# Five early expert rows of the first tile added by VectorE onto the residual, and one row given back to TensorE

## The reference

```
qry    = (x_blk @ w_query).reshape(T, 8, 2, 128)
scores = einsum('thpd,hpnd->thpn', qry, sub_keys)
top_s, top_i = top_k(scores, 16)              # for either half of the key
best_s, pos  = top_k(cand_s, 16)              # over the 16 x 16 sums
gate = softmax(best_s)
act  = gelu(einsum('thkd,td->thk', expert_u[idx], x_blk))
ff   = einsum('thk,thkd->td', gate * act, expert_v[idx])
h    = h + ff
```

## Time and profile before

| | |
|---|---|
| median of 3 runs | 1584.37 us (1582.99 to 1586.37) |
| the profiled execution, its own time | 1583.33 us |
| its span in the trace | 1581.4 us |
| busy: PE, DVE, ACT, POOL | 1346.1, 972.3, 537.5, 564.5 us |
| mean granted TensorE clock | 0.966 of full speed |
| read from HBM | 618.38 MB, mean 392 GB/s over the span |

### The profile page before, as it was taken

One profiled execution on the slowest core, in us unless ns is written; L12 is line 12 of the kernel. 1 busy time (PEld: TensorE's weight loads), 2 busy tenths in 40 slices (PEclk: granted clock), 3 DMA queues, 4 the chain that ended last, 5 costly groups with the idle time before them and its releaser, 6 DMA issues.

```text
span 1581.4 us, 14465 instructions
## 1 busy us (share of the span) xinstructions
PE 1346.1 (85%) x4096; PEld 664.7 (42%) x4096; DVE 972.3 (61%) x2428; ACT 537.5 (34%) x1638; POOL 564.5 (36%) x532
## 2 busy tenths in 40 slices
PE   7999899889776997889998699788899877777776
PEld 5555565445332443333555244333365432222222
DVE  3327598988774434763477856574557887554544
ACT  2324332323233223562323323564322323332322
POOL 1001345454442332444443333344444343333330
PEclk9999999999997999989999899999999999999998
DMA  9317999999999999999999999999999999999995
GB/s 380 145 53 293 377 408 421 421 421 420 421 421 422 421 420 422 419 402 410 421 421 420 422 420 421 421 405 396 422 421 420 421 421 421 423 421 422 421 422 212
DMA packets 85086, 620.39 MB, mean 392 GB/s; under 512 B 10352, under 2 KB 10352, under 8 KB 11280
## 3 DMA queue, kind: packets, MB, share of 16 engines
q0 software_dynamic: 74768, 551.65, 84.4%
q1 hardware_dynamic: 9792, 67.77, 10.4%
q10 hardware_dynamic: 448, 0.05, 0.0%
HBM read 618.38 MB, written 1.05 MB: 392 GB/s over the span
## 4 chain that ended last, share of the span: by engine, by line
PE 41%; DMA 39%; DVE 10%; ACT 7%; issue 3%; SPq 0%; POOL 0%; ACTq 0%; DVEq 0%; POOLq 0%
DMA arena<-in_peer_uv_dram,hnT 28%; PE banks L542 25%; PE banks L567 5%; PE banks L422 5%; DMA raw<-in_peer_uv_dram,hnT 5%; DMA work<-in_peer_uv_dram,hnT 4%; DVE arena L1422 3%; PE banks L688 2%; DMA rt<-in_diff_lambda_k_dram 2%; ACT g_e L930 2%; ACT hnT L919 1%; PE banks L514 1%; DVE raw L1422 1%; DVE work L1422 1%; ACT hnT L914 1%
## 5 line engine op out<-in xcount | busy, mean ns | idle before, releaser
L542 PE MATMUL banks<-arena,g_e 128*128 128x512 f32 x1184 | 575.5, 619 | 129.7 <-ACT g_e L930 128.7
L348 POOL DMA_INDIRECT arena<-in_peer_uv_dram,hnT x299 | 324.8, 1086 | 508.2 <-PE banks L542 498.4
L542 PEld LDWEIGHTS banks<-arena,g_e 128*128 128x128 f32 x1184 | 217.8, 196 | 404.8 <-issue 213.0
L1422 DVE CUSTOM_DVE_ANT_0 arena<-arena,hrows 128x1024 f32<-128x1024 f32 x209 | 253.9, 1222 | 153.9 <-DMA arena<-in_peer_uv_dram,hnT 149.8
L914 ACT ACTIVATE hnT<-hnT 128x2 f32<-128x2 f32 (+1 forms) x240 | 48.7, 203 | 697.0 <-DVE hnT L1422 692.2
L542 PE MATMUL banks<-raw,g_e 128*128 128x512 f32 x424 | 208.2, 622 | 41.3 <-ACT g_e L930 37.3
L348 POOL DMA_INDIRECT raw<-in_peer_uv_dram,hnT x106 | 115.8, 1092 | 178.2 <-PE banks L542 175.8
L930 ACT ACTIVATE g_e<-ident,hnT 128x128 f32<-128x128 f32 x501 | 172.7, 393 | 1.7 <-ACT hnT L919 0.6
L1422 DVE CUSTOM_DVE_ANT_0 arena<-arena,banks 128x1024 f32<-128x1024 f32 x90 | 109.6, 1220 | 85.4 <-DMA arena<-in_peer_uv_dram,hnT 85.3
L542 PEld LDWEIGHTS banks<-raw,g_e 128*128 128x128 f32 x424 | 78.3, 197 | 135.1 <-issue 78.4
L1422 DVE CUSTOM_DVE_ANT_0 raw<-raw,hrows 128x1024 f32<-128x1024 f32 x80 | 97.6, 1225 | 56.3 <-DMA raw<-in_peer_uv_dram,hnT 55.9
(11 more groups left out here) (236 smaller groups left out, 1299.5 us busy)
## 6 DMA issues: line engine op xcount, KB each, us to landing
arena<-in_diff_in_dram SPq DMA_DIRECT2D x24, 1024.0 KB
arena<-in_peer_query_dram SPq DMA_DIRECT2D x16, 1024.0 KB
arena<-in_gla_in_dram POOLq DMA_DIRECT2D x5, 2048.0 KB, 21.1
arena<-in_peer_query_dram SPq DMA_DIRECT2D x4, 2048.0 KB, 10.3
arena<-in_diff_out_dram SPq DMA_DIRECT2D x8, 1024.0 KB
arena<-in_peer_uv_dram,hnT POOLq DMA_INDIRECT x299
work<-in_gla_out_dram POOLq DMA_DIRECT2D x2, 2048.0 KB, 40.1
arena<-in_gla_in_dram SPq DMA_DIRECT2D x2, 1024.0 KB, 12.2
```

Source lines behind the costliest of these rows:

```text
L348: pool.indirect_dma_start(pair(n), None, table, bass.IndirectOffsetOnAxis(ap=places[:, o:o + 1].bitcast(u32), axis=0)).then_inc(S(f"pair_l ...
L542: last = nc.tensor.matmul(bank(2 * (tile % NT) + half), diags[:, slot * P:(slot + 1) * P], v_row(n)[:, half * 512:(half + 1) * 512], start ...
L1422: V.tensor_tensor_reduce(out=u_row(n), in0=u_row(n), in1=normed, scale=1.0, scalar=0.0, op0=ALU.mult, op1=ALU.add, accum_out=dots[:, o:o + ...
```

## The change

Rows 1, 3, 5, 7 and 9 join `ADDED`, and row 16 leaves it. Nothing else is edited, but everything that is computed from the list follows: the diagonals that ScalarE makes, the rows that TensorE sums, the semaphore and count on which the gathers 8, 10, 14, 16, 18 and 25 wait (these take over the buffers of rows 1, 3, 5, 7, 9 and 16), the wait of `add_experts`, and the slots of the diagonals.

```
--- before.py
+++ after.py
@@ -132,7 +132,7 @@
 
 
 HOME, TURNS, BEFORE = homes()
-ADDED = [n for n in range(16, 80, 6)]
+ADDED = [1, 3, 5, 7, 9] + [n for n in range(22, 80, 6)]
 SUMMED = [n for n in range(ROWS) if n not in ADDED]
```

## The result

The changed kernel took 1586.44 us, median of 22 runs (1583.98 to 1589.83), against 1583.74 us (1581.61 to 1589.21) for 22 runs of the kernel before: ratio 1.0018, 95% interval 1.0012 to 1.0023, so 2.9 us slower and just under the 0.2% taken as no change. The forecast was 1585.4 on a median of 1584.37, +1.1 us. The profiled execution took 1586.36 us with a span of 1584.3, 2.9 above the span of before.

The account below looks back on a forecast made before the run. The gathers' DMA stream up to about 226 us was taken as the bound. Gather 26's data flowing 0.8 us later and gather 27's 0.3 summed to +1.1 us: 1585.4 us on the median (+0.07%), range 1581.7 to 1587.8.

Parts of the forecast that it names:

- The adds cost nothing: VectorE's five added adds, 1.33 us each, 6.7 us in all, are covered by waits: 0 on the path.
- Their buffers, 0: Gather 10 waits for add 3 (165.0 instead of 163.16), gather 18 for add 9; nothing runs dry: 0.
- Rows 1, 3 and 9 save nothing: On TensorE these rows precede waits for diagonals, so removing them only leaves idle gaps of 5.3 and 3.1 us.
- Row 16, +1.72: Row 16 returns to TensorE in front of row 17 and puts rows 17, 18 and 19 1.72 us late.
- The price of a fall, 1.75 us: TensorE's half clock behind each new gap lasts four matmuls and costs 1.75 us; bounds nothing and 3.1 us.
- half clock for longer: Rival, chance 0.13: on TensorE the second gap, or both, costs 3.1 us instead of 1.75; 1586.8 to 1588.2 us.
- A rule weighed, nothing for the adds' effect on POOL: A gather inside an add took 0.94 us like others, so the skill's SBUF contention rule was priced at nothing.
- Nothing behind 226 us gives it back or adds: Behind 226 us the stream is full and VectorE slightly ahead, so the 1.1 us loss stays unchanged to the end.
- The clock does not pay: Rival, chance 0.13: TensorE's new gaps cost nothing, gathers 26 to 28 come 1.7 us earlier; 1582.2 us.
- only one gap pays: Rival, chance 0.17: on TensorE 1.75 of 3.44 us is lost and row 16 takes the rest; 1584.4 us.
- The stream fills: Rival, chance 0.06: earlier gathers around 18 fill the 353 GB/s stretch and its 3.6 us reach the end; 1580.8 us.
- The adds hold POOL: Rival, chance 0.03: adds 3, 7 and 9 each hold a gather 1.3 us, one without backlog; 1586.7 us.

Follow-up runs that it names:

- experiment 3: Kernel before with only rows 5 and 7, inside the query block, moved to VectorE: 1581.14 against 1583.61 us, ratio 0.9985.
- experiment 6: Changed kernel with both TensorE gaps filled by matmuls nobody reads (five calls behind row 2, three behind the scores): 1581.66 us against 1583.77 of before, ratio 0.9986.
- experiment 4: Kernel before with only row 16 given back to TensorE: 1585.70 against 1583.61 us, ratio 1.0011.
- experiment 1: Kernel before with only rows 1 and 3 moved to VectorE: 1585.98 against 1583.61 us, ratio 1.0014.
- experiment 5: Changed kernel with row 16 left on VectorE: 1585.76 us against 1583.77 of the kernel before, ratio 1.0010.
- experiment 2: Kernel before with only row 9 moved to VectorE: 1585.78 against 1583.61 us, ratio 1.0015.
- experiment 7: Changed kernel with only the first TensorE gap filled, by five matmul calls nobody reads: 1584.13 us against 1583.77 of the kernel before, ratio 0.9996.
- experiment 9: Kernel before with the last tile's dots reading their second operand from SBUF instead of PSUM: 1584.01 against 1583.77 us, ratio 0.9999.
- experiment 12: Kernel before with rows 5, 6, 7 and 8 moved to VectorE and two unread matmul calls behind row 3: 1580.89 against 1583.41 us, ratio 0.9983.
- experiment 11: Kernel before with rows 5, 6, 7 and 8, all inside the query block, moved to VectorE: 1580.81 against 1583.75 us, ratio 0.9984.
- experiment 8: Changed kernel with both TensorE gaps half filled by unread matmuls (three calls and one): 1583.32 us against 1583.75 of the kernel before, ratio 0.9996.

## Why the prediction had the sign right and the size too small

Sign and mechanism were right: +1.1 us predicted, +2.9 measured. That lies inside the whole range, which took in the rivals, and above the +0.3 to +1.9 that the sum gave itself. The size is wrong in the clock term, in what VectorE does to a gather's issue, and in gather 25, which was left out.

- **The adds cost nothing**: held. They ran at 154.10, 162.98, 168.84, 175.84 and 181.92 (predicted 154, 164, 169, 176, 182), 1.28 us each, and experiments 3 and 6 carry two and five of them and are faster than before. Only gather 13 starts inside one of them (176.72) and takes 1.21 us instead of 0.94.
- **Their buffers, 0**: held for the five rows. Gather 10 went at 164.53 (165 predicted), gather 18 at 187.07 instead of 191.49. The sum left out the buffer of row 16: gather 25 waits for TensorE and goes at 211.19 instead of 208.25, and in 210 to 212 the stream moves 262 GB/s instead of 401, ahead of gather 26.
- **Rows 1, 3 and 9 save nothing**: held. The gaps measured 4.85 and 3.07 us (5.3 and 3.1 predicted). The first is shorter because row 4 starts 0.5 us earlier in this execution (164.22 for 164.73). **Row 16, +1.72**: held for the gathers by the trace of experiment 4; its time, +1.7, is known only to 1.4.
- **The signs to look for**: the search came at 188.35 (188.5 predicted, in part by luck, as the 0.5 us of row 4 make up for a first fall of 2.1 instead of 1.75), gather 12 at 175.47 (175.6), both falls where they were expected; gathers 26 to 28 at 214.70, 217.51 and 219.46 instead of 214, 217 and 219.
- **The price of a fall, 1.75 us**: the mis-sized term. The half clock did not end with the four matmuls from which it was priced. First gap: row 4 took 3.57 us from start to start instead of 1.82, and the out block 7.24 instead of 6.87: 2.1 us. Second gap: rows 10 and 11 took 6.05 instead of 3.53: 2.5 us. In the other kernels' traces, worked out in the same way, a fall in the first gap cost 2.7 (experiment 1) and 2.9 us (5), one in the second 2.5 (2), 2.9 (5) and 3.0 (7). With the second fall at 2.5, rows 12 and 13 start at 196.80 instead of 196.12, and with row 16 gather 26 is 0.7 + 1.7 = 2.4 us late, not 1.7. The rival "half clock for longer" (1586.8 to 1588.2) had this mechanism. It priced the second fall at 3.1 us, against 2.5 here and up to 3.0 in experiment 7.
- **A rule weighed, nothing for the adds' effect on POOL**: this step failed. It rested on one gather, and it looked at the adds alone, while in this kernel it is dots that hold gathers 14, 26 and 28. Counted over the trace of before, none of 233 gathers that start with VectorE idle takes over 0.99 us; of 149 that start within a dot with both operands in SBUF 114 take over 1.1, up to 2.01, and none of 18 within a dot with one in PSUM over 0.95. Gather 26 of the kernel after starts at 214.70 inside a dot of 214.57 to 215.79, and ends at 216.61: 0.82 us behind the dot. Of the 127 gathers in before that a dot makes longer than 0.97 us, 125 end 0.79 to 0.83 us behind it. The Trainium skill, SBUF — State Buffer, "Who interferes with whom", says that a VectorE instruction with both inputs in SBUF contends with a GpSimd instruction that reads SBUF; by these counts and experiment 9 the trace agrees. The gather at 219.94 of the earlier trace rows is no case against it. It starts 0.07 us after the add, and the add takes 1.33 us where it takes 1.28 elsewhere. Seven gathers of before start within the first 0.04 us of a dot and take 0.94, and each of these dots takes 1.26 to 1.30 us instead of 1.22: here VectorE was held, by little. Other gathers that start as early are held themselves (gather 14 of the kernel after, at 178.23, 0.05 us into a dot: 1.98 us).
- **Corrected sum.** Gather 26's data flow 2.4 + 1.0 us later; 0.9 us was in hand: +2.5. Gather 27 is 2.4 late with 0.6 in hand, +1.8, and adds nothing. So +2.5 for a measured +2.9 (1.9 to 3.6). In the trace row 28's dot, which waits for its data in both kernels, starts at 228.32 instead of 225.16, 3.2 us later: the sum is 0.7 short there, and gather 25 is the term it lacks that the trace shows; its share was not measured. That the issue's 1.0 us is part of the result is worked out from the trace; no run took it away alone.
- **Nothing behind 226 us gives it back or adds**: not held in single executions. Against the one profiled execution of before, the kernel of experiment 3 leads by 4.5 us at gather 30, by 1.2 at gather 100 and by 0.6 at the last; the kernel after lags 1.1, 3.3 and 2.8. The timed gain of experiment 3 (2.4 us) is also less than its 4.5. Counted by the bytes of the gathers' queue, its stream is 3.5 us ahead of that of before from 240 to 366 us, and loses this only later, where the stream is not full. Windows, the first two of the kernel before, the others of experiment 3:

```profile
500.00:550.00 50.00, 44.68 (x106) 19.92 (x107) 24.41 (x47) 15.16 (x55) 16.05 (x17) 0.97 1.01 422
600.00:650.00 50.00, 37.95 (x104) 16.25 (x102) 26.62 (x54) 21.10 (x57) 17.33 (x15) 0.93 1.01 419
```

```profile
500.00:550.00 50.00, 45.97 (x109) 20.50 (x110) 23.27 (x43) 14.49 (x55) 15.54 (x16) 0.97 1.01 415
600.00:650.00 50.00, 37.89 (x102) 16.47 (x101) 25.92 (x53) 22.28 (x63) 16.94 (x15) 0.90 1.00 406
```

  These two stretches cost 2.4 us together. What holds the stream there stays open. The version of experiment 12 kept 4.0 of its 7.4 in the profiled execution, and was not faster than the others when timed.
- **The rivals.** "The clock does not pay" and "only one gap pays" are refuted by experiments 1, 2 and 6. "The stream fills" did not happen in the changed kernel (394 GB/s in 184 to 206), but describes experiments 3, 6, 11 and 12 (420 to 425). They gain 2.2 to 2.7 us of its 3.6. "Half clock for longer" comes nearest to what happened. "The adds hold POOL" named the right contention and the wrong instruction: it was a dot that held gather 26.

## What to carry to other kernels

Work taken from TensorE ahead of a wait buys no time but a longer gap, and the gap can halve the clock for what stands behind it; take it from inside a dense stretch (experiment 3: −2.4 us for two rows), or fill the gap with matmuls that nobody reads (experiment 6: 5.1 us for eight calls). Taking too much makes a new gap further on (experiment 11). Price a fall of the clock by the whole work that runs behind it until the durations are normal again, not by the first instruction. A rule about contention is weighed against a count over the trace, not against one instruction that happened to escape.

## What the runs showed of the hardware that was not expected

- In the stretch studied the clock fell behind 4.82 to 4.91 us (three traces) and 3.07 to 3.08 us of idle time (four traces), every time. Behind 2.24 and 2.38 us it fell too (experiments 8 and 9), behind 2.21 it did not (experiment 8), nor behind 2.51. Further on a gap of 2.12 us is followed by a fall in experiment 1 (first line: 3.33 us for four matmuls), and one of 3.08 us by none in experiment 6 (second line: 3.70 for eight):

```profile
298.90 3.33 PE L542 MATMUL banks<-raw,g_e 128*128 128x512 f32 x4 [2.12 <-ACT g_e L930]
```

```profile
324.32 3.70 PE L542 MATMUL banks<-work,g_e 128*128 128x512 f32 x8 [3.08 <-ACT g_e L941]
```

  The Trainium skill, TensorE: Matmul & The Clock Gate, "What's actually happening", calls the throttled state the default that activity lifts, and says that the chip watches a window that runs free of the kernel. The trace agrees with the first part: the granted clock is 0.50 behind the gaps and 1.00 again under work, and 1.98 us become 3.78, the levels of 1.2 and 2.4 GHz. The second would fit the gaps of nearly one length with both outcomes; no run here shows the window.
- The issue of an indirect gather on GpSimd takes 0.94 us alone and up to 2.03 (the kernel after) when it starts inside a VectorE dot with two SBUF operands; it then ends 0.81 us behind the dot. With the dots' second operand in PSUM 4 of 119 issues take over 1.1 us, and none of these four starts inside a dot.
